# Rotary part of a two-layer encoder kernel: from its own stage into the projection, and semaphores cleared by five engines

## The chip, the cores and the metric

One Trainium2 chip, one core of it. The time is what the device takes for one execution of the whole program, in microseconds (us). The kernel before took 4610.36 us in the median of three runs (4608.76 to 4613.35).

## What is computed

Two layers of an encoder on 2048 tokens of 1024 features, in float32. Each layer normalises, projects to 26 x 128 columns (and 16 more), and sends the columns through a gated delta net (12 tiles after a convolution, 4 gate tiles) and through attention with 8 query heads over 2 key heads of 64 dimensions (4 tiles of queries, one of keys, one of values, 4 of gates). What matters here is what happens to queries and keys between projection and attention:

```python
def _rmsnorm(x, w):
    y = x32 * lax.rsqrt(jnp.mean(x32 * x32, axis=-1, keepdims=True) + EPS)
    return (y * w.astype(jnp.float32)).astype(x.dtype)

def _rope(x, pos):
    ...
    rot = jnp.concatenate([-x32[..., d // 2:], x32[..., :d // 2]], axis=-1)
    return (x32 * cos + rot * sin).astype(x.dtype)

def _axial_rope(x, row, col):
    h = x.shape[-1] // 2
    return jnp.concatenate([_rope(x[..., :h], row), _rope(x[..., h:], col)], axis=-1)

    q = _axial_rope(_rmsnorm(q, q_norm_w), row, col)
    k = _axial_rope(_rmsnorm(k, k_norm_w), row, col)
```

With d = 32 in `_rope`, the 64 dimensions of a head fall into four quarters of 16: quarter 0 is rotated with 1, quarter 2 with 3.

## The kernel before

The program (`build`, L2022) is a chain of stages. Each stage opens its semaphores, runs one block in which SP (DMA queue), TensorE, ScalarE, VectorE and GpSimd each have their own list of instructions, and closes with a barrier. Stages do not overlap: `semaphores` (L52) lets all engines come to the end of the block, then clears every semaphore of the stage one after the other on SP (L58), then holds a barrier over all engines (L59). A layer is `input_projection` (L162), `token_inputs` (L450), `delta_net`, `attention`, `output_projection`, `token_scales`.

**input_projection.** Weights and activations are split into a high and a low float32r part, and a tile of 128 output columns x 2048 tokens is the sum of three products: per half tile (1024 tokens) 8 x 3 x 2 matmuls of 512 columns (`tile_half`, L242). Tiles go in the order values, queries, keys of the delta net (tiles 0 to 11, with a convolution on VectorE), attention queries (12 to 15), keys (16), values (17), gates (18 to 25). For tile t+1 ScalarE casts the high part of the weights (`split_hi`, L309) and VectorE subtracts for the low part (`split_w`, L374), each once tile t-1 is done; the weights have two buffers. ScalarE evicts each half tile from PSUM (`evacuate`, L314; `plain`, L335), SP stores the tile to DRAM (L212, the last two L216) and loads the weights of tile t+2 (L210). For tiles 4 to 17 GpSimd squares the tile (L296) and TensorE sums the squares over the 64 dimensions of each head with 16 small matmuls (`square_sum`, L259), put between the matmuls of the second half of tile t+2; the squares have one buffer. At the end VectorE copies the sums to SBUF (L425).

**token_inputs** computes decay and beta tables of the delta net from `ba` (a chain of some 25 small operations, with four transposed pieces of `v` copied by ScalarE, L584, ahead of the logarithm, L587), stores `b_rows` (L507) and, after the rotary rows, `att_v` (L515). The rotary part runs behind it in the same lists. Inverse root mean squares are taken (L595, L689), transposed, stored as rows to DRAM and loaded again as two rows per tile (L510 to L513). Then for each of 5 tiles: TensorE swaps the quarters with a permutation (`swap_quarters`, L554), VectorE makes two products with the norm weight and the tables (L705, L708), GpSimd adds them (L523), TensorE spreads the inverse over 128 partitions (L570), VectorE scales (L719), ScalarE casts the high part (L612), VectorE subtracts the low part (L696), and ScalarE's queue issues four stores of 64 partitions (L605). The loads of these tiles (L505), the swap matrix and the tables (L500 to L503) are issued at the beginning of the stage.

## Time and profile before

| | |
|---|---|
| median of 3 runs | 4610.36 us |
| profiled execution: time | 4615.77 us |
| profiled execution: span of the instructions | 4614.0 us |
| mean granted TensorE clock | 0.934 |
| TensorE busy | 4031.0 us (87%) |
| VectorE busy | 2615.2 us (57%) |
| ScalarE busy | 1869.3 us (41%) |
| GpSimd busy | 726.8 us (16%) |
| DMA | 418.01 MB, mean 91 GB/s |

The profile is of one execution of the program. PE is TensorE's matmuls, PEld its weight loads, DVE VectorE, ACT ScalarE, POOL GpSimd, SPq the queue on which SP issues DMAs. L-numbers are lines of the kernel. "x16" is a count of instructions. What stands in brackets behind an instruction of a timeline is how long its engine was idle before it and who released it. PEclk is the granted clock of TensorE as a share of 2.4 GHz, so 0.50 is 1.2 GHz. The first layer's input_projection ends and its token_inputs begins at 743.76 us from the start of the span.

### The profile page before, as it was taken

To read this page: it belongs to the slowest core of one execution; us is meant where nothing else is said; L and a number is where in the kernel's file an instruction comes from. 1 tells how busy PE (TensorE), PEld (TensorE's weight loads), DVE (VectorE), ACT (ScalarE), POOL (GpSimd) and SP (SyncE) were. 2 spreads that over 40 slices of the span, in tenths; PEclk is the share of its full clock that TensorE was granted. 3 is DMA by queue.
4 is the path that set the end of the run, shared out by engine and by line. 5 is a ranking of instruction groups with operands and counts; after the bars stand their busy time and mean duration, and the time that the engine had idled before them with its cause. 6 is when DMAs were issued, how large, how long until landed. Compare 5 with 4: busy or idle time off the path is not lost. (4 is left out here: it accounts for less than half of the span.)

```text
span 4614.0 us, 57747 instructions
## 1 busy us (share of the span) xinstructions
PE 4031.0 (87%) x19861; PEld 3102.9 (67%) x19861; DVE 2615.2 (57%) x3176; ACT 1869.3 (41%) x2596; POOL 726.8 (16%) x770
## 2 busy tenths in 40 slices
PE   3999997569979999987879999856997999999693
PEld 2788884359956666656758888725996666666473
DVE  5543003457778888874255500045676888888532
ACT  3221111235547777761132211112453777777310
POOL 0011101478510000000000110035863000000000
PEclk9999997789989999998989999967998999999896
DMA  6111113744520000017231111265455000000635
GB/s 238 62 69 68 55 69 128 172 115 135 150 76 21 23 23 23 23 47 206 105 127 69 55 68 69 76 182 136 122 148 129 24 23 23 22 23 16 166 135 205
DMA packets 319745, 418.01 MB, mean 91 GB/s; under 512 B 104336, under 2 KB 254212, under 8 KB 292428
## 3 DMA queue, kind: packets, MB, share of 16 engines
q1 hardware_dynamic: 315232, 386.57, 26.9%
q10 hardware_dynamic: 4352, 29.36, 2.4%
q8 instruction: 92, 1.51, 0.1%
q14 instruction: 69, 0.57, 0.0%
HBM read 267.95 MB, written 147.91 MB: 90 GB/s over the span
## 5 line engine op out<-in xcount | busy, mean ns | idle before, releaser
L1687 DVE TENSOR_REDUCE att_sb_part<-att_banks 128x1 f32<-128x512 f32 x992 | 658.8, 685 | 150.7 <-PE att_banks L1572 142.6
L1675 ACT ACTIVATE att_sb_probs<-att_banks 128x1024 f32<-128x1024 f32 x512 | 524.9, 1025 | 379.3 <-PE att_banks L1598 379.1
L1705 DVE TENSOR_TENSOR att_sb_p_lo<-att_sb_probs,att_sb_p_hi 128x1024 fp32r<-128x1024 f32 x512 | 623.6, 1218 | 22.6 <-ACT att_sb_p_hi L1679 20.5
L1679 ACT ACTIVATE att_sb_p_hi<-att_sb_probs 128x1024 fp32r<-128x1024 f32 x512 | 543.3, 1061 | 16.2
L254 PE MATMUL proj_banks<-proj_sb_h_hi,proj_sb_w_hi 128*128 128x512 f32 x1600 | 518.3, 405 | 6.2 <-DVE proj_sb_w_lo L376 6.2
L254 PE MATMUL proj_banks<-proj_sb_h_lo,proj_sb_w_hi 128*128 128x512 f32 x1600 | 515.6, 403 | 0.0
L254 PE MATMUL proj_banks<-proj_sb_h_hi,proj_sb_w_lo 128*128 128x512 f32 x1600 | 515.5, 403 | 0.0
L376 DVE TENSOR_TENSOR proj_sb_w_lo<-proj_sb_w_raw,proj_sb_w_hi 128x1024 fp32r<-128x1024 f32 x52 | 69.2, 1330 | 640.8 <-ACT proj_sb_w_hi L312 640.8
L996 PE MATMUL dn_banks<-dn_sb_room 128*128 128x128 f32 x3072 | 379.8, 283 | 59.6 <-DMA dn_sb_room<-proj 28.3
L996 PEld LDWEIGHTS dn_banks<-dn_sb_room 128*128 128x128 f32 x3072 | 367.8, 198 | 82.2 <-DMA dn_sb_room<-proj 38.5
L1614 PE MATMUL att_banks<-att_sb_p_hi,att_sb_v_hi 128*65 128x512 f32 x1024 | 406.7, 397 | 12.7 <-DVE att_sb_o L1711 11.3
L1597 PE MATMUL att_banks<-att_sb_q,att_sb_k 128*128 128x512 f32 x1024 | 413.1, 403 | 2.8 <-DVE att_sb_q L1699 1.9
L296 POOL TENSOR_TENSOR proj_sb_sq<-proj_sb_out 128x2048 f32<-128x2048 f32 x28 | 100.8, 3600 | 1976.5 <-ACT proj_sb_out L333 1388.1
L1598 PE MATMUL att_banks<-att_sb_q,att_sb_k 68*128 68x512 f32 x1024 | 409.1, 399 | 0.0
L1614 PE MATMUL att_banks<-att_sb_p_hi,att_sb_v_lo 128*65 128x512 f32 x1024 | 404.3, 395 | 0.0
L1614 PE MATMUL att_banks<-att_sb_p_lo,att_sb_v_hi 128*65 128x512 f32 x1024 | 403.5, 394 | 0.0
L1572 PE MATMUL att_banks<-att_sb_k,att_sb_q 128*128 128x512 f32 x992 | 380.9, 413 | 7.2 <-DVE att_sb_part L1687 1.9
L254 PEld LDWEIGHTS proj_banks<-proj_sb_h_hi,proj_sb_w_hi 128*128 128x128 f32 x1600 | 289.4, 189 | 65.0 <-issue 7.1
L254 PEld LDWEIGHTS proj_banks<-proj_sb_h_hi,proj_sb_w_lo 128*128 128x128 f32 x1600 | 291.4, 189 | 60.7
L254 PEld LDWEIGHTS proj_banks<-proj_sb_h_lo,proj_sb_w_hi 128*128 128x128 f32 x1600 | 291.4, 189 | 60.7
L317 ACT ACTIVATE proj_sb_out<-proj_banks 128x1024 f32<-128x1024 f32 x56 | 57.4, 1026 | 566.1 <-PE proj_banks L254 566.1
L1572 PEld LDWEIGHTS att_banks<-att_sb_k,att_sb_q 128*128 128x128 f32 x992 | 189.1, 191 | 121.4 <-DVE att_sb_part L1687 65.7
(225 smaller groups left out, 5748.9 us busy)
## 6 DMA issues: line engine op xcount, KB each, us to landing
proj<-proj_sb_out SPq DMA_DIRECT2D x52, 1024.0 KB, 4.4
dn_sb_kq<-proj SPq DMA_DIRECT2D x64, 512.0 KB, 5.3
proj_sb_w_raw<-in_w_in SPq DMA_DIRECT2D x52, 516.0 KB, 5.2
dn_sb_room<-proj SPq DMA_DIRECT2D x32, 768.0 KB, 5.2
att_sb_q<-att_q SPq DMA_DIRECT2D x64, 256.0 KB, 2.9
out_sb_x<-x_res SPq DMA_DIRECT2D x16, 1024.0 KB, 7.0
x_res<-out_sb_x SPq DMA_DIRECT2D x16, 1024.0 KB, 4.1
out_sb_w_raw<-in_w_out SPq DMA_DIRECT2D x24, 512.0 KB, 4.9
```

Source lines behind the costliest of these rows:

```text
L254: mm = nc.tensor.matmul(ps[:, 2 * half + n, :], w[:, u, k, :], h[:, k, at:at + QB], start=(k == 0 and w is w_hi and h is h_hi), stop=(k == ...
L296: nc.gpsimd.tensor_tensor(sq[:], out[:, u, :], out[:, u, :], ALU.mult).then_inc(s["squared"], 1)
L376: nc.vector.tensor_tensor(w_lo[:, u].rearrange("p k m -> p (k m)"), w_raw[:, u, 0:KT * P], w_hi[:, u].rearrange("p k m -> p (k m)").bitcas ...
L996: mm = nc.tensor.matmul(out[:, h, :], left[:, h, :], right[:, h, :], start=True, stop=True)
L1572: nc.tensor.matmul(ps[:, 4 + u % 2, :], q1[:, slot, tile * P:(tile + 1) * P], k1[:, slot % 2, keys * QB:(keys + 1) * QB], start=True, stop ...
L1597: nc.tensor.matmul(out, k1[:, slot % 2, keys], q1[:, slot, :], start=True, stop=False)
L1598: mm = nc.tensor.matmul(out, k2[:, slot % 2, keys], q2[:, slot, :], start=False, stop=True)
L1614: mm = nc.tensor.matmul(ps[0:DH + 1, 6, :], part_v[:, kv, tile, :], part_p[:, at, m, :], start=opens, stop=(tile == NC - 1 and part_v is v ...
L1675: nc.scalar.activation(probs[:, pair % 2], ps[:, 2 * (pair % 2):2 * (pair % 2) + 2, :], ACT.Exp, scale=SCALE).then_inc(s["exp_done"], 1)
L1679: nc.scalar.activation(p_hi[:, pair % SLOTS], probs[:, pair % 2], ACT.Copy).then_inc(s["hi_done"], 1)
L1687: nc.vector.tensor_reduce(part[:, w // NQ, w % NQ:w % NQ + 1], ps[:, 4 + w % 2, :], AX.X, ALU.max) \
L1705: nc.vector.tensor_tensor(p_lo[:, pair % SLOTS], probs[:, pair % 2], p_hi[:, pair % SLOTS].bitcast(F32), ALU.subtract).then_inc(s["lo_done ...
```

## The change

1. The rotary part leaves `token_inputs` and goes into `input_projection`. The columns of queries and keys are laid out anew on the host: tile 12 holds quarters 0 and 2 of heads 0 to 3 and tile 13 their quarters 1 and 3, likewise 14 and 15 for heads 4 to 7, and 16 and 17 for the two key heads, whose upper 64 partitions hold half of the values each. A rotation then needs no permutation: it is between two tiles at the same partition.
2. A unit is 512 tokens of a pair of tiles; there are 3 pairs x 4 = 12 units. VectorE does all of it: four products, an addition, a scaling by rows broadcast from DRAM, a copy to the high part, a subtraction for the low part. Units 0 and 1 stand behind the weight split beside tile 20, then 3, 3, 2, 2 beside tiles 21 to 24. Inputs (`ab`, `inv`) and results (`xx`, `yy`) have two buffers each, in the space of `pad` and `sq`; the tables (`rope`) one.
3. SP stores and loads for the units between its weight loads and tile stores.
4. The square sums have four columns (one for each 32 partitions) in place of two. Those of tile 16 go between the matmuls of the first half of tile 18, those of tile 17 into its second half; the inverse roots are taken after tile 18, transposed by TensorE between the halves of tile 19, and stored and loaded as before.
5. `token_inputs` keeps the rest: 13 semaphores for 31. `input_projection` has 47 for 28.
6. In every stage the semaphores are cleared in turn by SP, VectorE, ScalarE, GpSimd and TensorE, each its own share.

```diff
+STATS = T_Z - T_Q
+QUARTER = P // 4
+PAIR_TILES = 3
+N_ROWS = ATT_HEADS + KV_HEADS
+ROPE_UNITS = PAIR_TILES * NQ
+ROPE_TILE = T_Z + 2
+UNITS_BESIDE = (2, 3, 3, 2, 2, 0)
+FIRST_BESIDE = (0, 2, 5, 8, 10, 12)
...
-        for s in sems.values():
-            nc.sync.sem_clear(s)
+        engines = (nc.sync, nc.vector, nc.scalar, nc.gpsimd, nc.tensor)
+        for n, s in enumerate(sems.values()):
+            engines[n % len(engines)].sem_clear(s)
...
+                def load_unit(n):
+                    if n >= ROPE_UNITS:
+                        return
+                    pair, at, parts = rope_unit(n)
+                    u = n % 2
+                    cols = slice(at, at + QB)
+                    if n >= 2:
+                        sp.wait_ge(s["scaled"], n - 1)
+                    sp.dma_start(ab[u][0:parts], a.proj[T_AQ + 2 * pair:T_AQ + 2 * pair + 2, 0:parts, cols]
+                                 .rearrange("f p t -> p f t")).then_inc(s[f"ab_loaded{u}"], 16)
+                    heads = parts // QUARTER
+                    sp.dma_start(inv[u][0:parts], a.qk_rows[4 * pair:4 * pair + heads, cols].unsqueeze(1)
+                                 .broadcast_to([heads, QUARTER, QB])).then_inc(s[f"inv_loaded{u}"], 16)
+
+                def load_rope(n):
+                    if n % PAIR_TILES == 0 and n < ROPE_UNITS:
+                        if n:
+                            sp.wait_ge(s["products"], n)
+                        cols = slice(rope_unit(n)[1], rope_unit(n)[1] + QB)
+                        sp.dma_start(rope, a.rope[:, :, cols].rearrange("f p t -> p f t")).then_inc(s["rope_loaded"], 16)
+
+                def store_unit(n):
+                    pair, at, parts = rope_unit(n)
+                    u = n % 2
+                    heads = parts // QUARTER
+                    dst = a.att_q[4 * pair:4 * pair + heads] if pair < PAIR_TILES - 1 else a.att_k
+                    for src, low in ((yy[u], 0), (xx[u], DH)):
+                        sp.wait_ge(s["lo" if low else "hi"], n + 1)
+                        for half in range(2):
+                            row = low + half * QUARTER
+                            sp.dma_start(dst[:, row:row + QUARTER, at:at + QB], src[0:parts, half, :]) \
+                                .then_inc(s[f"rope_stored{u}"], 16)
+
+                t = ROPE_TILE - 2
+                load_weights(t)
+                store_tile(t)
+                load_weights(t + 1)
+                sp.wait_ge(s["rows_copied"], 2)
+                rows_out = a.qk_rows.rearrange("r (c p) -> (r c) p", p=P)
+                sp.dma_start(rows_out[0:P], row_table[:, 0, :]).then_inc(s["rows_stored"], 16)
+                sp.dma_start(rows_out[P:N_ROWS * NC], row_table[0:N_ROWS * NC - P, 1, :]).then_inc(s["rows_stored"], 16)
+                sp.wait_ge(s["rows_stored"], 32)
+                load_rope(0)
+                load_unit(0)
+                load_unit(1)
+                for t in range(ROPE_TILE, N_TILES):
+                    load_weights(t)
+                    store_tile(t - 1)
+                    for n in range(FIRST_BESIDE[t - ROPE_TILE], FIRST_BESIDE[t - ROPE_TILE] + UNITS_BESIDE[t - ROPE_TILE]):
+                        load_rope(n + 1)
+                        store_unit(n)
+                        load_unit(n + 2)
+                store_tile(N_TILES - 1)
...
-                    col = (t - T_Q) * 2 * NC + 2 * n
-                    mm = nc.tensor.matmul(ps[:, 4, bass.ds(col, 2)], sq[:, n * P:(n + 1) * P], c.halves[:],
+                    col = (t - T_Q) * 4 * NC + 4 * n
+                    mm = nc.tensor.matmul(sums[:, bass.ds(col, 4)], sq[:, n * P:(n + 1) * P], c.quarters[:],
...
-                with pe.Fori(T_Q // 2 + 1, T_Z // 2 + 1) as i:
+                with pe.Fori(T_Q // 2 + 1, T_Z // 2) as i:
                     for u in range(2):
                         tile_half(i, u, 0)
 
-                        tile_half(i, u, 1, [lambda n=n: square_sum(i - 1, u, n) for n in range(NC)])
+                        tile_half(i, u, 1, [[lambda n=n: square_sum(i - 1, u, n)] for n in range(NC)])
+                i = T_Z // 2
+                tile_half(i, 0, 0, [[lambda n=n: square_sum(i - 1, 0, n)] for n in range(NC)])
+                late = [[]] * 12 + [[lambda n=n: square_sum(i - 1, 1, n)] for n in range(8)]
+                late += [[lambda n=n: square_sum(i - 1, 1, n), lambda n=n: square_sum(i - 1, 1, n + 1)] for n in range(8, NC, 2)]
+                tile_half(i, 0, 1, late)
+                tile_half(i, 1, 0)
+                pe.wait_ge(s["inv_rms"], 1)
+                nc.tensor.transpose(ps[:, 6, 0:P], rms_flat[:, 0:P], c.ident[:])
+                nc.tensor.transpose(ps[0:N_ROWS * NC - P, 7, 0:P], rms_flat[:, P:N_ROWS * NC], c.ident[:]) \
+                    .then_inc(s["turned"], 1)
+                tile_half(i, 1, 1)
...
+                plain(T_Z // 2, 0, ACT.Silu, True, True)
+                act.wait_ge(s["summed"], 2)
+                nc.scalar.activation(rms.rearrange("p m r c -> p m c r"), first_sums, ACT.Sqrt, bias=c.eps[:, 0:1],
+                                     scale=1.0 / DH).then_inc(s["root"], 1)
+                plain(T_Z // 2, 1, ACT.Silu, True, True)
+                for t in range(ROPE_TILE, N_TILES):
+                    plain(t // 2, t % 2, ACT.Silu, t + 1 < N_TILES)
...
+                def inverse_rms():
+                    att_sums = sums[:, (T_AQ - T_Q) * 4 * NC:STATS * 4 * NC] \
+                        .rearrange("p (m f c r) -> p m f c r", m=PAIR_TILES, f=2, r=4)
+                    dve.wait_ge(s["stats_done"], STATS)
+                    nc.vector.tensor_copy(first_sums, att_sums[:, :, 0]).then_inc(s["summed"], 1)
+                    dve.wait_ge(s["summed"], 1)
+                    nc.vector.tensor_tensor(first_sums, att_sums[:, :, 1], first_sums, ALU.add).then_inc(s["summed"], 1)
+                    nc.vector.tensor_reduce(c.sums[:].rearrange("p t c -> p (t c)"),
+                                            sums[:, 0:2 * DN_HEADS * 4 * NC].rearrange("p (n r) -> p n r", r=4),
+                                            AX.X, ALU.add).then_inc(s["edges"], 1)
+                    dve.wait_ge(s["root"], 1)
+                    nc.vector.reciprocal(rms_flat, rms_flat).then_inc(s["inv_rms"], 1)
+
+                def copy_rows():
+                    dve.wait_ge(s["turned"], 1)
+                    nc.vector.tensor_copy(row_table[:, 0, :], ps[:, 6, 0:P]).then_inc(s["rows_copied"], 1)
+                    nc.vector.tensor_copy(row_table[0:N_ROWS * NC - P, 1, :], ps[0:N_ROWS * NC - P, 7, 0:P]) \
+                        .then_inc(s["rows_copied"], 1)
+
+                def rope_products(n):
+                    pair, _, parts = rope_unit(n)
+                    u, k = n % 2, int(pair == PAIR_TILES - 1)
+                    w_first, w_second, w_negative = 2 * k, 2 * k + 1, 4 + k
+                    dve.wait_ge(s[f"ab_loaded{u}"], 16 * (n // 2 + 1))
+                    dve.wait_ge(s["rope_loaded"], 16 * (n // PAIR_TILES + 1))
+                    if n >= 2:
+                        dve.wait_ge(s[f"rope_stored{u}"], 64 * (n // 2))
+                    for dst, half, src, weight, table in ((xx, 0, 0, w_first, 0), (yy, 0, 1, w_negative, 1),
+                                                           (xx, 1, 1, w_second, 0), (yy, 1, 0, w_first, 1)):
+                        op = nc.vector.scalar_tensor_tensor(out=dst[u][0:parts, half, :], in0=ab[u][0:parts, src, :],
+                                                            scalar=qk_w[0:parts, weight:weight + 1],
+                                                            in1=rope[0:parts, table, :], op0=ALU.mult, op1=ALU.mult)
+                    op.then_inc(s["products"], 1)
+
+                def rope_rest(n):
+                    parts, u = rope_unit(n)[2], n % 2
+                    x, y = xx[u][0:parts], yy[u][0:parts]
+                    dve.wait_ge(s["products"], n + 1)
+                    nc.vector.tensor_tensor(x, x, y, ALU.add).then_inc(s["added"], 1)
+                    dve.wait_ge(s["added"], n + 1)
+                    dve.wait_ge(s[f"inv_loaded{u}"], 16 * (n // 2 + 1))
+                    factor = inv[u][0:parts].unsqueeze(1).broadcast_to([parts, 2, QB])
+                    nc.vector.tensor_tensor(x, x, factor, ALU.mult).then_inc(s["scaled"], 1)
+                    dve.wait_ge(s["scaled"], n + 1)
+                    nc.vector.tensor_copy(y.bitcast(F32R), x).then_inc(s["hi"], 1)
+                    dve.wait_ge(s["hi"], n + 1)
+                    nc.vector.tensor_tensor(x.bitcast(F32R), x, y, ALU.subtract).then_inc(s["lo"], 1)
+
+                split_w(T_Z + 1, 1)
+                inverse_rms()
+                split_w(T_Z + 2, 0)
+                copy_rows()
+                dve.wait_ge(s["qk_w_loaded"], 16)
+                nc.vector.tensor_scalar(qk_w[:, 4:6], qk_w[:, 1:4:2], -1.0, None, ALU.mult).then_inc(s["edges"], 1)
+                dve.wait_ge(s["edges"], 4)
+                for t in range(ROPE_TILE, N_TILES):
+                    if t + 1 < N_TILES:
+                        split_w(t + 1, (t + 1) % 2)
+                    for n in range(FIRST_BESIDE[t - ROPE_TILE], FIRST_BESIDE[t - ROPE_TILE] + UNITS_BESIDE[t - ROPE_TILE]):
+                        rope_products(n)
+                        rope_rest(n)
...
+                for kv in range(KV_HEADS):
+                    sp.dma_start(v[kv * DH:(kv + 1) * DH], a.proj[T_AK + kv, DH:P]).then_inc(s["v_loaded"], 16)
```

## Rows read from the trace of the kernel before

**Rows 1.** Windows: busy PE, PEld, DVE, ACT, POOL; clock; DMA; GB/s.
```profile
601.00:736.00 135.00, 135.00 (x578) 108.53 (x577) 6.67 (x6) 17.56 (x17) 0.00 (x0) 1.00 0.17 62
743.00:770.00 27.00, 10.47 (x44) 7.90 (x45) 9.55 (x30) 10.08 (x17) 0.00 (x0) 0.56 0.87 334
...
840.00:857.00 17.00, 0.00 (x0) 0.00 (x0) 0.00 (x0) 0.14 (x1) 0.14 (x1) 0.50 0.73 185
...
1400.00:1500.00 100.00, 98.88 (x418) 65.88 (x417) 88.58 (x115) 73.50 (x71) 0.00 (x0) 1.00 0.08 23
```

**Rows 2.** Timeline of SP's queue, first layer: start us, duration us, issue.
```profile
737.61 0.34 SPq L216 DMA_DIRECT2D proj<-proj_sb_out  x1
743.76 0.33 SPq L496 DMA_DIRECT2D tab_sb_ba<-ba  x1
...
745.51 0.42 SPq L499 DMA_DIRECT2D tab_sb_v<-proj  x1
...
762.79 0.33 SPq L507 DMA_DIRECT2D b_rows<-tab_sb_rows  x1
...
856.87 0.35 SPq L944 DMA_DIRECT2D dn_sb_masks<-in_masks  x1
```

**Rows 3.** The same, second layer.
```profile
2989.45 0.33 SPq L496 DMA_DIRECT2D tab_sb_ba<-ba  x1
...
3008.83 0.33 SPq L507 DMA_DIRECT2D b_rows<-tab_sb_rows  x1
...
3102.74 0.35 SPq L944 DMA_DIRECT2D dn_sb_masks<-in_masks  x1
```

**Rows 4.** Timeline of ScalarE in token_inputs.
```profile
755.76 0.58 ACT L584 COPY tab_sb_vt<-tab_banks 128x512 f32<-128x512 f32 x1 [0.24 <-PE tab_banks L536]
...
757.66 0.31 ACT L587 ACTIVATE tab_sb_ln<-tab_sb_u 128x128 f32<-128x128 f32 x1
```

**Rows 5.** Timeline of TensorE in token_inputs.
```profile
752.07 3.65 PE L536 MATMUL tab_banks<-c_ident,tab_sb_v 128*128 128x128 f32 x16 [1.27 <-DMA tab_sb_v<-proj]
...
766.62 0.48 PE L549 MATMUL tab_banks<-c_ident,tab_sb_att_inv 128*128 128x128 f32 x1 [4.38 <-DVE tab_sb_att_inv L689]
```

**Rows 6.** DMA issues: count, KB each, median us to landing.
```profile
dn_o<-dn_sb_room SPq DMA_DIRECT2D x32, 256.0 KB, 2.5
...
qk_rows<-tab_sb_rows SPq DMA_DIRECT2D x2, 64.0 KB, 1.7
```

**Rows 7.** The four last tile stores (L216), issue to landing.
```profile
DMA to landing us min/median/max: 3.8/3.9/3.9
```

**Rows 8.** Semaphore clears (L58): all, after input_projection, after token_inputs.
```profile
L58 SPq EVENT_SEMAPHORE_RANGE_CLEAR  x442: 25/25/35, 3.9 to 4613.7; - x148
...
L58 SPq EVENT_SEMAPHORE_RANGE_CLEAR  x28: 25/28/30, 741.9 to 743.5; - x28
...
L58 SPq EVENT_SEMAPHORE_RANGE_CLEAR  x31: 25/25/30, 854.8 to 856.6; - x31
```

**Rows 9.** Timelines: GpSimd, squares of tile 16; ScalarE, evictions.
```profile
545.45 3.60 POOL L296 TENSOR_TENSOR proj_sb_sq<-proj_sb_out 128x2048 f32<-128x2048 f32 x1 [22.33 <-PE proj_banks L265]
...
549.72 1.03 ACT L317 ACTIVATE proj_sb_out<-proj_banks 128x1024 f32<-128x1024 f32 x1 [13.66 <-PE proj_banks L254]
...
575.64 1.03 ACT L317 ACTIVATE proj_sb_out<-proj_banks 128x1024 f32<-128x1024 f32 x1 [13.58 <-PE proj_banks L254]
...
601.57 1.03 ACT L317 ACTIVATE proj_sb_out<-proj_banks 128x1024 f32<-128x1024 f32 x1 [13.58 <-PE proj_banks L254]
```

**Rows 10.** Instruction forms of VectorE: count, busy us, mean ns, idle.
```profile
L1705 DVE TENSOR_TENSOR att_sb_p_lo<-att_sb_probs,att_sb_p_hi 128x1024 fp32r<-128x1024 f32 x512 | 623.6, 1218 | 22.6 <-ACT att_sb_p_hi L1679 20.5
...
L416 DVE TENSOR_SCALAR proj_sb_out<-proj_sb_pad,proj_sb_taps 128x2048 f32<-128x2048 f32 x24 | 30.9, 1287 | 191.1 <-ACT proj_sb_pad L317 191.1
...
L708 DVE SCALAR_TENSOR_TENSOR tab_sb_q<-tab_sb_q,tab_sb_qk_w,tab_sb_rope 128x2048 f32<-128x2048 f32 x10 | 23.4, 2343 | 0.0
L1400 DVE SCALAR_TENSOR_TENSOR dn_sb_room<-dn_banks,dn_sb_norm,dn_sb_room 128x512 f32<-128x512 f32 x32 | 22.9, 748 | 38.3 <-PE dn_banks L1072 38.3
```

More of the change, by code:

```diff
@@ L166, in input_projection @@
              "conv_step taps_kept conv_done out_ready out_stored0 out_stored1 ba_hi ba_split ba_stored edges "
-             "squared stats_done")
+             "squared stats_done summed root inv_rms turned rows_copied rows_stored qk_w_loaded rope_loaded "
+             "ab_loaded0 ab_loaded1 inv_loaded0 inv_loaded1 products added scaled hi lo rope_stored0 rope_stored1")
     with ExitStack() as stack, semaphores(nc, names) as s:
@@ L212, in _, with load_weights, store_tile @@
                         sp.dma_start(a.proj[t], out[:, u, :]).then_inc(s[f"out_stored{u}"], 16)
+                def load_weights(t):
+                    if t + 2 < N_TILES:
+                        sp.wait_ge(s["w_lo"], t + 1)
+                        sp.dma_start(w_raw[:, t % 2, :], a.w_in[l, t + 2]).then_inc(s[f"w_loaded{t % 2}"], 16)
+                def store_tile(t):
+                    sp.wait_ge(s["out_ready"], t + 2)
+                    sp.dma_start(a.proj[t], out[:, t % 2, :]).then_inc(s[f"out_stored{t % 2}"], 16)
@@ L213, in _ @@
                 for u in range(2):
[L214 to L216 removed]
+                    sp.wait_ge(s[f"rope_stored{u}"], 64 * (ROPE_UNITS // 2))
                 for u in range(2):
@@ L250, in tile_half @@
                             if between:
-                                between.pop(0)()
+                                for extra in between.pop(0):
+                                    extra()
                             for n in range(2):
@@ L439, in scratch @@
     a.d_blk = dram("d_blk", (2, NC, N_DIR, DN_HEADS, N_BLK, BLK, BLK))
-    a.qk_rows = dram("qk_rows", (N_QK * 2, SEQ))
+    a.qk_rows = dram("qk_rows", (N_ROWS, SEQ))
     a.att_q = dram("att_q", (ATT_HEADS, P, SEQ))
@@ L450, in token_inputs @@
 def token_inputs(nc, a, c, l):
-    names = ("loaded ba_turned act_step dve_step summed g_copied turned copied stored att_root "
-             "const_loaded rows_loaded v_loaded v_turned v_copied v_stored swapped spread "
-             "cos_done sin_done rotated scaled hi lo stored0 stored1 " + " ".join(f"x_loaded{t}" for t in range(N_QK)))
+    names = "loaded ba_turned act_step dve_step summed g_copied turned copied stored v_loaded v_turned v_copied v_stored"
     n_ba = 2 * ITEMS
@@ L516, in _ @@
                 sp.wait_ge(s["v_stored"], 16)
-            @block.gpsimd
-            def _(pool):
-                for t in range(N_QK):
-                    pool.wait_ge(s["sin_done"], t + 1)
-                    pool.wait_ge(s["cos_done"], t + 1)
-                    nc.gpsimd.tensor_tensor(q[:, t, :], q[:, t, :], sin_part[:, t % 2, :], ALU.add).then_inc(s["rotated"], 1)
             @block.tensor
@@ L1984 @@
     pass
+FIRST_DIMS = [*range(0, DH // 4), *range(DH // 2, 3 * DH // 4)]
+SECOND_DIMS = [d + DH // 4 for d in FIRST_DIMS]
 def constants():
@@ L2034, in build @@
         c.eps = sb("c_eps", [P, 2])
-        c.halves = sb("c_halves", [P, 2])
-        c.sums = sb("c_sums", [P, T_Z - T_Q, NC, 2])
+        c.quarters = sb("c_quarters", [P, 4])
+        c.sums = sb("c_sums", [P, 2 * DN_HEADS, NC])
         c.tok = sb("c_tok", [P, TABLES, NC, ITEMS])
@@ L2068 @@
 _SHAPES = ["x_in", "w_in", "w_ba", "norm_w", "decay", "dn_norm_w", "qk_norm_w", "w_out",
-           "masks", "ident", "ones", "halves", "rope", "quarter", "swap", "halves_t"]
+           "masks", "ident", "ones", "quarters", "rope", "quarter"]
 def lay_out(x, norm_w, w_in, conv_w, a_log, dt_bias, dn_norm_w, q_norm_w, k_norm_w, w_out, final_norm_w):
@@ L2095, in lay_out @@
     g["dn_norm_w"] = np.asarray(dn_norm_w)[:, :, None]
-    swap = np.arange(DH).reshape(4, DH // 4)[[1, 0, 3, 2]].reshape(-1)
-    q, k = np.asarray(q_norm_w), np.asarray(k_norm_w)
-    g["qk_norm_w"] = np.stack([np.concatenate([v, v], axis=1) for v in (q, q[:, swap], k, k[:, swap])], axis=2)
+    norm_cols = []
+    for v in (np.asarray(q_norm_w), np.asarray(k_norm_w)):
+        first, second = np.tile(v[:, FIRST_DIMS], (1, 4)), np.tile(v[:, SECOND_DIMS], (1, 4))
+        norm_cols += [first, second]
+    g["qk_norm_w"] = np.stack(norm_cols, axis=2)
     g["w_out"] = np.asarray(w_out).reshape(depth, KT, P, KT, P).transpose(0, 3, 2, 1, 4).reshape(depth, KT, P, KT * P)
```

176 lines of the change are left out of this document (42 added, 134 removed).

## The prediction

> **What bounds the kernel now.** I read the windows first, to see which stage leaves TensorE idle. In the projection's last tiles TensorE is busy all of the 135 us at a clock of 1.00, VectorE 6.67 us and the DMA engines 17% [rows 1]. In the stage after it, the one that the change takes apart, TensorE has 10.47 us of work in the first 27 us at a clock of 0.56, and the last 17 us hold nothing but DMA [rows 1]. Then the SP queue's timeline, for the stage's length: it opens with the load of `ba` at 743.76 and the next stage's first issue is at 856.87, 113.1 us; in the second layer 2989.45 and 3102.74, 113.3 us [rows 2, 3]. The store of `b_rows`, the last thing that does not belong to the rotary part except the store of `att_v`, is issued 19.0 and 19.4 us after the start [rows 2, 3]. So some 94 us of each layer are rotary work and its stores, serial, with TensorE nearly idle, while VectorE idles beside the projection. The two layers run in sequence, so a microsecond off a stage is a microsecond off the time.
>
> **Part 1: the stage without its rotary part.** The b_rows store waits for a chain through ScalarE: the four copies of the turned `v` end at 755.76 + 0.58 and the logarithm follows at 757.66 [rows 4]. TensorE began to turn `v` at 752.07, after 1.27 us of waiting for its load, issued at 745.51 [rows 5, 2]. Without 7 MB of rotary loads on the queue, and with `v` in two halves issued back to back, I let that wait vanish: 1.1 us, and nearly 1.5 in the second layer. b_rows goes out at 17.9 us. It lands after some 1.9 us (the like-sized qk_rows store: 1.7 [rows 6]), at 19.8; SP only then issues `att_v`, 1 MB like a projection tile, whose last store lands in 3.9 us [rows 7]; with 0.3 for the wake-up of SP, 24.0. The last projection store shows what follows a landing: issued 737.61, landed 3.9 later, first semaphore clear at 741.9, so 0.4 us; the last clear at 743.5, the stage at 743.76, so 0.25 [rows 2, 7, 8]. With three clears in a row (below), 24.0 + 0.4 + 0.2 + 0.25 = 24.9 us. Saved: 88.2 + 88.4 = 176.6 us. Bounds: the stage takes no less than 23 us (`v` early by 2 us) and no more than 33 (both stores with 4 us more each, if what slowed them behind the rotary loads were not those loads): 160 to 180.
>
> **Part 2: the clears.** 31 clears span 854.8 to 856.6 and 28 span 741.9 to 743.5, 0.058 us each; 442 run in all [rows 8]. Other engines have stopped by then, so every one is on the path. After the change the projection has 47 names for 28 and the small stage 13 for 31; dealt to five engines and rounded up stage by stage, the longest share adds to 97. 345 fewer in series are 20.0 us, of which 2 x 28 x 0.058 = 3.2 are in part 1: 16.8 us. No row shows a clear on another engine. If TensorE's or GpSimd's took twice as long, the 97 cost 11.2 instead of 5.6; if they cost so much that nothing is won, 0. I take SP's pace, the only row, and keep 0 to 17.
>
> **Part 3: what the projection takes on.** TensorE: two transposes, 0.48 us for one [rows 5], between the halves of tile 19: 0.9 us a layer. The square sums stay 16 a tile; with them a tile takes 601.57 - 575.64 = 25.93 us [rows 9], without 22.5 (six tiles in the 135 us of [rows 1]), and four output columns for two I cost at nothing, between 0 and the 3.4 us that one tile's 16 sums add. They are earlier: tile 16's now start with tile 18. Its squares begin on GpSimd at 545.45 and take 3.60, so 549.05; tile 17's last eviction starts 549.72 [rows 9], so they are ready with under 0.5 us to spare; bound 0 to 0.5 a layer. Tile 17's squares follow at about 564, six us ahead of their first sum. inverse_rms: after tile 18, four small VectorE operations and a root with its table loads on ScalarE, some 5 us against 11.25 until the transposes: hidden under half a tile. Sum: 2 x 0.9 = 1.8 us, bounds 0 and 9.
>
> VectorE: a unit is four products of 512 columns, 0.75 us each (0.748, the nearest row, though it reads PSUM), two full-width operations and a subtraction of 1024, 1.22 each, and a copy of 1024, 0.69 (half of the single-source 1.287 for 2048) [rows 10]: 7.35 us. Twelve are 88 us, for 46 us of the same work in 2048-column operations (5 x 4 x 2.3) [rows 10]: smaller instructions cost more, but off the path.
>
> What covers it: unit 0 starts some 3.7 us into tile 20, behind the eviction, the ScalarE split and split_w(21). Three units and a split are 23.4 us, longer than a tile's 22.5, but split_w(t+1) is due only when tile t ends. split_w(23) stands behind five units: 3.7 + 5 x 7.35 + 1.3 = 42 us, w_hi at 48, due at 67.5. split_w(25) stands behind ten units and four splits: 83 us of work, due at 112.5. It holds until a unit costs (112.5 - 8.9) / 10 = 10.4 us, 8.9 being the 3.7 and four splits of 1.3 (1.22 and the start). SP: per unit three loads at most and four stores, seven DMAs at 0.35 to 0.6 us of issue; the load of weights t+2 and the store of tile t-1 stand in front of each tile's units, and the next ones behind them, so a late unit delays a weight load by a few us of the 16 it has (22.5 less its landing).
>
> DMA: a full unit moves 0.75 MB in and 1 MB out, eight full and four half ones, four rotary tables of 0.5 MB, and five tiles of 1.5 MB: 28 MB. The stores at 840 to 857 ran at 185 GB/s for a share of 0.73, 253 GB/s at full; the loads at 743 to 770 at 334 for 0.87, 384 at full [rows 1]. So 74 to 112 us of DMA beside 135 us of six tiles: tight at the lower rate, hidden at both, and the sum takes nothing for it. The Trainium skill (DMA: Bandwidth & Descriptors, "Bandwidth") speaks against 256 KB pieces: it asks for transfers of 1 MiB or more and gives each DMA about 2 us fixed, by itself an estimated 14 us for the seven of a unit. The rows say that what is fixed overlaps: 334 GB/s over 27 us with `v` and what follows issued half a microsecond apart. What the time would be if it did not is rival (d).
>
> **Sum.** 176.6 + 16.8 - 1.8 = 191.6 us off the profiled execution's 4615.8: 4424.2. That execution lies 5.4 us over the median of the runs, 4610.4, so I expect a median near 4420.
>
> **Rivals.**
> (a) The clears gain little, since other engines clear slowly or the barrier after them eats it: the change then does only part of what it says. Against it stand short semaphore instructions on all; for it, that no row shows one. 16.8 us back: 4437. 8%.
> (b) The delta net after the stage starts with another clock history: TensorE is idle for the last 17 us before it, at 0.50 [rows 1], so I expect the same start; a shift of 5 us a layer either way gives 4410 or 4430. 7%.
> (c) The units, not TensorE, set the end: the DMA chain of a unit (stores, then the next loads of the same buffers behind them in the queue) makes a unit cost 12 us for 7.35. Past 10.4 us each microsecond costs ten a layer: 2 x 16 = 32 us, 4452. For it: the 112 us above. 4%.
> (d) The queue takes one DMA at a time. With 2.5 us for a 256 KB store [rows 6] and 4 for the 0.5 MB load (the 1 MB store's 3.9 [rows 7]) a unit costs 16.5 us: 61 us a layer until tile 25 may start, 4542. Against it: the SP queue issued `v` and the loads behind it half a microsecond apart and 27 us ran at 334 GB/s [rows 1, 2]. 1%.
> (e) Slower: with VectorE, ScalarE, DMA and TensorE all busy in tiles 20 to 24 the granted clock falls to its lower level, 0.50. Five tiles of 22.5 us become 45: 225 us in both layers, 4645. It turns the gain into a loss from 95 of the 112.5 us of a layer at half clock. Against it: attention has TensorE 98.88 and VectorE 88.58 busy of 100 us at 1.00 [rows 1]. 2%.
>
> **How the numbers follow.** The forecast, units hidden and clears at SP's pace, has 78%. Its own range is 4410 to 4434: at its low end the stage takes 23 us and nothing is taken on (197 us off), at its high end half of the distance to each upper bound is used up (168 + 14 - 5, 177 off). The range that holds eight in ten reaches to (a) with a stage some us longer: 4406 to 4444. A measurement of this kernel tells 0.2%, 9 us, from no change. Only (e) and accidents reach there: faster 0.97, same 0.01, slower 0.02.
>
> **What would show it.** In the profile after: the small stage 23 to 27 us from its first issue to the next stage's; VectorE over 70% busy in tiles 20 to 24 while TensorE stays at 100% and 1.00; evictions there still 11.25 us apart; SP with at most 17 clears in the largest stage. I am wrong in the mechanism if TensorE waits there for w_lo or the spacing grows; wrong in a size if the stage stays above 30 us or clears on another engine run for over 0.1 us each.

## The result, and the profile after

| | before | changed |
|---|---|---|
| median | 4611.85 us (4608.76 to 4613.75, 4 runs) | 4552.77 us (4548.33 to 4555.85, 4 runs) |
| ratio | | 0.9868, interval 0.9854 to 0.9883 |
| profiled execution: span | 4614.0 us | 4551.2 us |
| mean granted TensorE clock | 0.934 | 0.936 |
| TensorE / VectorE busy | 4031.0 / 2615.2 us | 3938.0 / 2696.9 us |

Faster, by 59 us or 1.3%, well outside the spread of the runs. I forecast 190 us and a range that ended at 4444; the result lies more than 100 us above it.

The SP queue of the changed kernel, first layer and then second, gives the stages (start us, duration us, issue; L644 opens the small stage, L989 the delta net):

```profile
779.38 2.98 SPq L253 DMA_DIRECT2D proj<-proj_sb_out  x2
797.06 0.33 SPq L644 DMA_DIRECT2D tab_sb_ba<-ba  x1
...
817.49 0.33 SPq L650 DMA_DIRECT2D b_rows<-tab_sb_rows  x1
819.04 0.33 SPq L653 DMA_DIRECT2D att_v<-tab_sb_vt  x1
823.86 0.34 SPq L989 DMA_DIRECT2D dn_sb_masks<-in_masks  x1
...
3016.02 0.33 SPq L644 DMA_DIRECT2D tab_sb_ba<-ba  x1
...
3044.14 0.34 SPq L989 DMA_DIRECT2D dn_sb_masks<-in_masks  x1
```

Against [rows 2, 3] the span divides like this:

| us | first projection ends | small stage 1 | between | small stage 2 | rest |
|---|---|---|---|---|---|
| before | 743.8 | 113.1 | 2132.6 | 113.3 | 1511.3 |
| changed | 797.1 | 26.8 | 2192.2 | 28.1 | 1507.1 |
| difference | +53.3 | -86.3 | +59.6 | -85.2 | -4.2 |

The small stages gave 171.5 of the 176.6 us forecast. The two projections (the second lies in "between") took 113 back, where I had written 1.8. So it is the term of the projection that failed (what the clears give lies inside these figures; e4 measures it). Where inside the projection, the windows show (columns as in [rows 1]):

```profile
600.00:620.00 20.00, 20.00 (x87) 16.07 (x86) 15.27 (x17) 1.70 (x2) 0.00 (x0) 1.00 0.36 130
660.00:700.00 40.00, 28.47 (x122) 22.37 (x120) 19.55 (x21) 4.01 (x4) 0.00 (x0) 0.89 0.42 151
700.00:750.00 50.00, 26.68 (x100) 21.05 (x101) 23.55 (x26) 2.99 (x3) 0.00 (x0) 0.74 0.40 139
```

For 20 us all is as forecast: TensorE full at 1.00, VectorE at three quarters. From 660 to 750 TensorE is busy some 60% of the time, and VectorE half of it: neither is the bound. The DMA engines show 40% of their time and 140 to 150 GB/s, which looks like room to spare. ScalarE's timeline says what is late:

```profile
654.72 1.03 ACT L422 ACTIVATE proj_sb_out<-proj_banks 128x1024 f32<-128x1024 f32 x1 [9.06 <-PE proj_banks L348]
665.91 1.03 ACT L422 ACTIVATE proj_sb_out<-proj_banks 128x1024 f32<-128x1024 f32 x1 [10.16 <-PE proj_banks L348]
688.83 1.04 ACT L417 CAST proj_sb_w_hi<-proj_sb_w_raw 128x1024 fp32r<-128x1024 f32 x1 [21.90 <-DMA proj_sb_w_raw<-in_w_in]
...
736.01 1.05 ACT L417 CAST proj_sb_w_hi<-proj_sb_w_raw 128x1024 fp32r<-128x1024 f32 x1 [42.77 <-DMA proj_sb_w_raw<-in_w_in]
...
769.82 1.03 ACT L422 ACTIVATE proj_sb_out<-proj_banks 128x1024 f32<-128x1024 f32 x1 [29.40 <-DMA proj<-proj_sb_out]
```

Evictions are 11.2 us apart until 665.91. Then ScalarE sits idle 22 and 43 us until the load of a weight tile lands and it can be split, and 29 us until the store that frees the buffer of an eviction has landed. TensorE waits 34.9 us for the low part of the weights, which comes behind that split. VectorE's units show the same. The first took 7.15 us, from its start to the next one's. Later VectorE waits nine times for inputs of a unit, 72 us in all, and 43.8 us of that are three waits for the rotary table; two of them are shown:

```profile
601.92 0.75 DVE L559 SCALAR_TENSOR_TENSOR proj_sb_pad<-proj_sb_pad,proj_sb_qk_w,proj_sb_small 128x512 f32<-128x512 f32 x1
...
609.07 0.75 DVE L559 SCALAR_TENSOR_TENSOR proj_sb_pad<-proj_sb_pad,proj_sb_qk_w,proj_sb_small 128x512 f32<-128x512 f32 x1
...
645.42 0.75 DVE L559 SCALAR_TENSOR_TENSOR proj_sb_pad<-proj_sb_pad,proj_sb_qk_w,proj_sb_small 128x512 f32<-128x512 f32 x1 [13.89 <-DMA proj_sb_small<-in_rope]
...
692.62 0.75 DVE L559 SCALAR_TENSOR_TENSOR proj_sb_pad<-proj_sb_pad,proj_sb_qk_w,proj_sb_small 128x512 f32<-128x512 f32 x1 [15.02 <-DMA proj_sb_small<-in_rope]
```

Why the loads are late stands in SP's queue. An issue takes some 0.4 to 0.6 us for one DMA when the queue takes it freely (a line with "x2" is two in a row); here they stretch:

```profile
607.92 1.22 SPq L285 DMA_DIRECT2D att_q<-proj_sb_sq  x2
609.19 1.80 SPq L285 DMA_DIRECT2D att_q<-proj_sb_pad  x2
611.04 2.75 SPq L263 DMA_DIRECT2D proj_sb_pad<-proj  x1
...
632.82 2.24 SPq L285 DMA_DIRECT2D att_k<-proj_sb_sq  x2
635.10 9.70 SPq L285 DMA_DIRECT2D att_k<-proj_sb_pad  x2
```

```profile
proj<-proj_sb_out SPq DMA_DIRECT2D x6, 1024.0 KB, 12.9
...
proj_sb_w_raw<-in_w_in SPq DMA_DIRECT2D x3, 516.0 KB, 12.4
```

The first store of a unit is issued at 607.92, and by the third unit two 128 KB stores occupy SP for 9.7 us. The queue is backed up from its far end: a tile store lands after 12.9 us (second fence: the DMA view from 600 to 797; count, KB each, median us to landing), where it took 3.9 before [rows 7]. A queue that is full while its 16 engines are busy 40% of the time suggests that the work is not spread over the 16. Short windows show it directly:

```profile
619.00:625.00 6.00, 6.00 (x28) 4.81 (x27) 1.81 (x3) 2.08 (x2) 0.00 (x0) 1.00 0.26 99
699.00:705.00 6.00, 0.00 (x0) 0.00 (x0) 1.48 (x2) 0.00 (x0) 0.00 (x0) 0.50 0.25 84
736.00:739.00 3.00, 2.09 (x9) 1.34 (x8) 0.00 (x0) 1.57 (x2) 0.00 (x0) 1.00 0.12 49
```

In the first two SP is issuing stores of queries, in the third stores of keys. A share of 0.25 is 4 engines of 16, full, and one of 0.12 is 2; per engine that makes 21 to 25 GB/s. In the second of them TensorE does nothing at all.

What is peculiar to the new DMAs is their shape. A store goes to `dst[:, row:row + 32, cols]`: outermost are 4 heads (2 for the keys), then 32 rows. The load of the inverse roots is a broadcast, also with 4 or 2 outermost. Before, a store went to 64 rows of one head. The Trainium skill ("DMA: Bandwidth & Descriptors", section "Why a DMA increments its semaphore by 16 and not by 1") says that a DMA is spread over the largest number up to 16 that divides the outermost dimension of both sides, and over the lowest-numbered engines. For these stores that is 4 for the queries and 2 for the keys, and the shares of 0.26 and 0.12 agree. The trace does not number the engines, so which ones they are no run here shows. The rule was in reach when I predicted and I did not apply it.

The clears of the changed kernel, after the first delta net (the window 1250 to 1254):

```profile
L73 POOLq EVENT_SEMAPHORE_RANGE_CLEAR  x17: 38/38/38, 1251.2 to 1252.2; - x17
L73 ACTq EVENT_SEMAPHORE_RANGE_CLEAR  x17: 41/41/43, 1251.2 to 1252.3; - x17
L73 SPq EVENT_SEMAPHORE_RANGE_CLEAR  x17: 25/25/25, 1251.2 to 1252.1; - x17
L73 DVEq EVENT_SEMAPHORE_RANGE_CLEAR  x17: 54/54/56, 1251.3 to 1253.0; - x17
L73 PEldq EVENT_SEMAPHORE_RANGE_CLEAR  x16: 56/56/56, 1251.3 to 1253.1; - x16
```

SP's pace is 0.056 us (0.9 us for 16 steps), VectorE's 1.7/16 = 0.11 and TensorE's 1.8/15 = 0.12. If the longest share goes by VectorE's pace, it comes to an estimated 97 x 0.11 = 10.7 us.

### The profile page after: what moved, and what is told of

Its sections match the earlier page's. It is cut to its first block and busy times, and to the rows that moved or that the text cites. A ratio compares the mean times of both kernels' runs of the same rounds, so it can differ in the third digit from the quotient of the medians.

```text
span 4551.2 us, 57469 instructions
## 1 busy us (share of the span) xinstructions
PE 3938.0 (87%) x19701; PEld 3070.6 (67%) x19701; DVE 2696.9 (59%) x3334; ACT 1856.8 (41%) x2590; POOL 671.2 (15%) x760
## 5 line engine op out<-in xcount | busy, mean ns | idle before, releaser
L1659 PE MATMUL att_banks<-att_sb_p_hi,att_sb_v_hi 128*65 128x512 f32 x1024 | 406.4, 397 | 12.6 <-DVE att_sb_o L1756 11.2
```

The costliest lines, as they stand in the source:

```text
L1659: mm = nc.tensor.matmul(ps[0:DH + 1, 6, :], part_v[:, kv, tile, :], part_p[:, at, m, :], start=opens, stop=(tile == NC - 1 and part_v is v ...
```

## The experiments

Theory A: the stores and the loads of the inverse roots run on 4 or 2 of the 16 engines, because 4 or 2 entries are outermost, and those engines set the pace of the stage. Theory B: what costs is the number, the size or the plain volume of the added DMAs on one queue. Theory C, in two of the expectations, is that the broadcast load of the inverse roots alone holds the queue. e1, e2, e3 and e7 change only the form of those DMAs in the changed kernel, e5 the layout too. The kernel before ran beside them: 4608.41 us (7 runs) beside e1, e2, e3 and e5, and 4607.97 us (12 runs) beside e4, e6, e7 and e9. Ratios are to these. Differences to the changed kernel's 4552.77 are between medians; by the ratios they are 2 to 8 us smaller.

**e1: the stores into rows in a line.** The rows of a store are contiguous in one dimension of 128 (or 64); the places are not those of the heads, so attention reads other data, and the roots are made 100 times larger so that its exponentials stay small.

```diff
+                    dst = dst.rearrange("h p t -> (h p) t")
...
-                            row = low + half * QUARTER
-                            sp.dma_start(dst[:, row:row + QUARTER, at:at + QB], src[0:parts, half, :]) \
+                            row = (2 * (low > 0) + half) * parts
+                            sp.dma_start(dst[row:row + parts, at:at + QB], src[0:parts, half, :]) \
...
-                                     scale=1.0 / DH).then_inc(s["root"], 1)
+                                     scale=1e4 / DH).then_inc(s["root"], 1)
```

> The four stores of a unit keep their number, bytes and 2 KB rows, but the destination is 128 (64) rows in a line instead of 4 (2) heads x 32 rows, so that its outermost size is 128. Rows land in the wrong place, and the roots are taken 100 times larger so that the scores stay finite. Theory A (a DMA is spread over as many of the 16 engines as its outermost size on both sides allows: 4 and 2 in the change): the first two engines carry 2.5 MB in place of 5.0 MB over these tiles, which at 22 to 25 GB/s each is 100 to 113 us, under the 135 us of six tiles; TensorE no longer waits and the time falls from 4553 to 4430 to 4440. Theory B (256 KB transfers of 2 KB rows, seven to a unit, are slow whatever their shape): 4553, unchanged. Theory C (the broadcast load of the inverse roots is what holds the queue): 4553, unchanged.

Measured: 4435.98 us (4429.58 to 4437.28), ratio 0.9625 [0.9609, 0.9641]. The same bytes in as many DMAs of the same sizes and 2 KB pieces, and 117 us less: volume, number and size are excluded as the main cause, and so is theory C, which expected 4553. The rows do land at other places in DRAM here; e7 below, with the places unchanged, excludes these too.

**e2: the inverse roots alone.** One row is broadcast to all 128 partitions in place of four rows to 32 each (heads 1 to 3 of a tile get head 0's factors).

```diff
-                    sp.dma_start(inv[u][0:parts], a.qk_rows[4 * pair:4 * pair + heads, cols].unsqueeze(1)
-                                 .broadcast_to([heads, QUARTER, QB])).then_inc(s[f"inv_loaded{u}"], 16)
+                    sp.dma_start(inv[u][0:parts], a.qk_rows[4 * pair, cols].partition_broadcast(parts)) \
+                        .then_inc(s[f"inv_loaded{u}"], 16)
```

> Only the load of the inverse roots changes: one row broadcast to 128 (64) partitions in place of 4 (2) rows broadcast to 32 each, with the same bytes, so every head is scaled by the first head's roots. Theory A: the first two engines carry 4.4 MB for 5.0, 13% less, and the stretch of the units shrinks by some 24 us a layer: 4500 to 4510. Theory B: 4553. Theory C: near 4435.

Measured: 4506.64 us (4498.32 to 4521.56), ratio 0.9786 [0.9761, 0.9811]: 46 us less (38 by the ratios), with the stores still narrow. That is in theory A's range and far from the 4435 of theory C.

**e3: both edits, and the roots as in e1.**

> Both edits together: rows land in the wrong place, every head is scaled by the first head's roots, and the roots are taken 100 times larger. Theory A: the bytes spread over all engines, 74 to 87 us of DMA beside 135 us, 4425 to 4440, little or nothing under the run with the stores alone. Theory B: 4553.

Measured: 4434.11 us (4430.96 to 4439.35), the ratio of e1. Once the stores are wide, the narrow loads cost nothing: what counts is whether the busiest engine is done in time, not each DMA by itself.

**e5: the whole computation, interleaved.** The columns are laid out so that partition 4r + h of a tile holds dimension r of head h. The outermost dimension of stores and broadcasts is then the 32 rows, the heads stand inside. The key tiles carry the values in two head places beside the two key heads, and the units take these places along; `v` is loaded in four pieces. Cut here: tables, norm weights, key columns and the load of `v`, which follow the layout.

```diff
-                            sp.dma_start(dst[:, row:row + QUARTER, at:at + QB], src[0:parts, half, :]) \
+                            sp.dma_start(dst[:, row:row + QUARTER, at:at + QB].rearrange("h r t -> r h t"), src[:, half, :]) \
...
-                    sp.dma_start(inv[u][0:parts], a.qk_rows[4 * pair:4 * pair + heads, cols].unsqueeze(1)
-                                 .broadcast_to([heads, QUARTER, QB])).then_inc(s[f"inv_loaded{u}"], 16)
+                    sp.dma_start(inv[u], a.qk_rows[4 * pair:4 * pair + 4, cols].unsqueeze(0)
+                                 .broadcast_to([QUARTER, 4, QB])).then_inc(s[f"inv_loaded{u}"], 16)
...
-            parts += [at_q + h * DH + np.array(dims) for h in range(head, head + 4)]
+            parts += [at_q + h * DH + np.array([d]) for d in dims for h in range(head, head + 4)]
```

> A full computation: partition 4r + h holds dimension r of head h (before: 32h + r), so the stores go to 32 rows x 4 heads and the roots come as 32 (repeated) x 4 rows, with 32 outermost. The key pair takes 128 partitions like the others, values included, which adds 3.5 MB. Theory A: 4425 to 4445, TensorE at 100% beside the units, evictions 11.25 us apart. Theory B: 4553 or a little more, for the added bytes.

Measured: 4431.53 us (4423.46 to 4434.91), ratio 0.9615 [0.9599, 0.9631]. Its window, two issues of SP, and what landed from 600 to 744:

```profile
600.00:735.00 135.00, 135.00 (x578) 108.53 (x577) 90.27 (x101) 17.58 (x17) 0.00 (x0) 1.00 0.67 230
```
```profile
611.69 1.29 SPq L285 DMA_DIRECT2D att_q<-proj_sb_sq  x2
613.02 1.27 SPq L285 DMA_DIRECT2D att_q<-proj_sb_pad  x2
...
744.40 0.33 SPq L644 DMA_DIRECT2D tab_sb_ba<-ba  x1
```
```profile
proj<-proj_sb_out SPq DMA_DIRECT2D x7, 1024.0 KB, 4.8
...
att_q<-proj_sb_sq SPq DMA_DIRECT2D x16, 256.0 KB, 2.5
...
proj_sb_w_raw<-in_w_in SPq DMA_DIRECT2D x3, 516.0 KB, 6.2
```

TensorE is busy in all 135 us at 1.00 beside 90 us of VectorE, the picture forecast; a 256 KB store lands in 2.5 us and the small stage begins at 744.40, 0.6 us later than before the change. It moves more bytes than the changed kernel (the two extra head places of the key units) and takes 121 us less.

**e6: the narrow shape in the kernel before.** Another stage, another queue (ScalarE's), larger DMAs:

```diff
-                    for half in range(2):
-                        head = (2 * t if t < N_QK - 1 else 0) + half
-                        part = slice(half * DH, (half + 1) * DH)
-                        for src, at in ((hi, 0), (lo, DH)):
-                            act.dma_start(dst[head, at:at + DH], src[part, t % 2, :].bitcast(F32)) \
-                                .then_inc(s[f"stored{t % 2}"], 16)
+                    head = 2 * t if t < N_QK - 1 else 0
+                    for src, at in ((hi, 0), (lo, DH)):
+                        act.dma_start(dst[head:head + 2, at:at + DH], src[:, t % 2, :].bitcast(F32)) \
+                            .then_inc(s[f"stored{t % 2}"], 16)
```

> The kernel before, where only the rotary stores differ: the two heads of a tile go out in one DMA of 1 MB (destination 2 heads x 64 rows) in place of two of 512 KB; half as many DMAs, twice as large, same bytes, same 8 KB pieces. Theory A (a DMA whose outermost dimension has 2 entries runs on 2 of the 16 engines): 10.5 MB a layer over two engines at 22 to 25 GB/s each are 210 to 240 us from about 790 us on, where the stage ended at 857; 140 to 170 us more a layer, 4890 to 4950. Theory B (the number or the size of DMAs is what costs): the same or a little faster than before, 4600 to 4612.

Measured: 4906.36 us (4905.0 to 4912.14), ratio 1.0648 [1.0632, 1.0664]; the stage takes 262.3 us for 113.1. Half as many DMAs of twice the size make the kernel 298 us slower. The window of its stores, where nothing else moves, and then the same stretch of the kernel before:

```profile
800.00:1000.00 200.00, 20.00 (x30) 7.07 (x28) 23.25 (x11) 6.04 (x4) 11.56 (x3) 0.52 0.12 52
```
```profile
800.00:857.00 57.00, 22.61 (x35) 8.01 (x33) 24.89 (x11) 7.42 (x5) 14.87 (x4) 0.59 0.80 184
```

A share of 0.12 is 2 engines of 16, full; 52 GB/s are 26 for each of them. The rule of the Trainium skill named above ("DMA: Bandwidth & Descriptors", the same section) gives 2 for this shape, and the trace agrees.

**e7: the layout kept, the DMAs cut by head.** Each has 32 rows outermost, 64 KB; a full unit has 21 DMAs in place of 6, and the output is whole.

```diff
-                    sp.dma_start(inv[u][0:parts], a.qk_rows[4 * pair:4 * pair + heads, cols].unsqueeze(1)
-                                 .broadcast_to([heads, QUARTER, QB])).then_inc(s[f"inv_loaded{u}"], 16)
+                    for h in range(heads):
+                        sp.dma_start(inv[u][h * QUARTER:(h + 1) * QUARTER],
+                                     a.qk_rows[4 * pair + h, cols].partition_broadcast(QUARTER)) \
+                            .then_inc(s[f"inv_loaded{u}"], 16)
...
-                            sp.dma_start(dst[:, row:row + QUARTER, at:at + QB], src[0:parts, half, :]) \
-                                .then_inc(s[f"rope_stored{u}"], 16)
+                            for h in range(heads):
+                                sp.dma_start(dst[h, row:row + QUARTER, at:at + QB],
+                                             src[h * QUARTER:(h + 1) * QUARTER, half, :]) \
+                                    .then_inc(s[f"rope_stored{u}"], 16)
```

> The changed kernel, its layout kept; each store of a unit and each load of inverse roots is cut into one DMA per head (32 rows x 512, 64 KB), so that a full unit has 21 DMAs in place of 6. The output is whole. Theory A (fan-out): every DMA now has 32 entries outermost and runs on 16 engines; 21 issues of some 0.4 us are 8.4 us a unit, still under the 11 us that a unit may take: 4430 to 4450. Theory B (each DMA costs a fixed time on the queue, small ones are bad): more than three times as many DMAs make the stage longer than in the changed kernel, 4600 or more.

Measured: 4448.44 us (4442.38 to 4449.2), ratio 0.9646 [0.9631, 0.9661]: at the upper end of theory A's range, and 104 us faster than the changed kernel with more than three times as many DMAs, and with every row written to the same place. Of the 17 us to e5 some 13 lie in the two projections, where the issues take longer:

```profile
610.18 3.63 SPq L292 DMA_DIRECT2D att_q<-proj_sb_sq  x8
613.85 4.61 SPq L292 DMA_DIRECT2D att_q<-proj_sb_pad  x8
```

Sixteen stores take SP 8.2 us, twelve more than e5 issues, and weights behind them come late once more (ScalarE is idle 14.6 us before one split of the first layer, until the load lands); the small stage begins at 750.53, 6 us after e5's. The rest lies in the small stages and behind them and is not explained.

**e4: the clears alone, in the kernel before.**

```diff
-        for s in sems.values():
-            nc.sync.sem_clear(s)
+        engines = (nc.sync, nc.vector, nc.scalar, nc.gpsimd, nc.tensor)
+        for n, s in enumerate(sems.values()):
+            engines[n % len(engines)].sem_clear(s)
```

> The kernel before with nothing changed but the clears, dealt to five engines. My forecast, 345 clears less in series at SP's 0.058 us each: 20 us off, 4590. By the rows of the changed kernel, where VectorE and TensorE take 0.11 us for one: 25.7 us of clears before against some 10.7 now, 15 us off, 4595. Rival (a) of the prediction, nothing is won: 4608 to 4612.

Measured: 4597.26 us (4589.86 to 4605.61, 8 runs) against 4607.97, ratio 0.9978 [0.9967, 0.9988]: 10 us, between 5.5 and 15. That nothing is won (rival (a)) is excluded, and so are the 20 us of SP's pace on every engine; the 15 us that the slower engines' pace gives are at the edge of the interval.

**e9: e5 with another order in the small stage.**

```diff
+                sp.wait_ge(s["v_copied"], NQ)
+                sp.dma_start(a.att_v.rearrange("p c k d -> p c (k d)"), vt[:]).then_inc(s["v_stored"], 16)
                 sp.wait_ge(s["copied"], 1)
                 sp.dma_start(a.b_rows.rearrange("c i t -> (c i) t"), rows[:]).then_inc(s["stored"], 16)
                 sp.wait_ge(s["stored"], 16)
-                sp.wait_ge(s["v_copied"], NQ)
-                sp.dma_start(a.att_v.rearrange("p c k d -> p c (k d)"), vt[:]).then_inc(s["v_stored"], 16)
...
+                act.wait_ge(s["dve_step"], 6)
+                nc.scalar.activation(ln[:], u[:], ACT.Ln).then_inc(s["act_step"], 1)
                 for n in range(NQ):
                     act.wait_ge(s["v_turned"], n + 1)
                     nc.scalar.copy(vt[:, n * NQ:(n + 1) * NQ, :].rearrange("p c d -> p (c d)"), ps[:, NQ + n, :]) \
                         .then_inc(s["v_copied"], 1)
-                act.wait_ge(s["dve_step"], 6)
-                nc.scalar.activation(ln[:], u[:], ACT.Ln).then_inc(s["act_step"], 1)
```

> The interleaved version (e5) with another order in the small stage alone: ScalarE takes the logarithm before the four copies of v instead of behind them, and att_v is stored ahead of b_rows instead of after b_rows has landed. If the stage is set by the late v, the copies behind it and two stores in a row: b_rows goes out 4 to 5 us earlier, att_v 6 us earlier, the stage takes 19 to 21 us for 26.5: 11 to 15 us off e5's 4431, 4416 to 4420. Rival: the two stores side by side slow each other, or the logarithm's table load only moves: 4426 to 4431.

Measured: 4416.84 us (4412.88 to 4420.37), ratio 0.9581 [0.9568, 0.9594]; it is the fastest version, 3% under the changed kernel. Its SP queue in the small stage:

```profile
744.23 0.33 SPq L644 DMA_DIRECT2D tab_sb_ba<-ba  x1
...
758.08 0.35 SPq L653 DMA_DIRECT2D att_v<-tab_sb_vt  x1
760.00 0.34 SPq L655 DMA_DIRECT2D b_rows<-tab_sb_rows  x1
763.15 0.33 SPq L992 DMA_DIRECT2D dn_sb_masks<-in_masks  x1
```

The stage takes 18.9 us for e5's 26.5: b_rows goes out 15.8 us after the start for 20.0, and the large store is under way before it. Two orders were changed at once, so what each gives alone is not shown.

## Why the prediction was wrong, step by step

**The step that failed** is the paragraph on DMA in Part 3: "So 74 to 112 us of DMA beside 135 us of six tiles: tight at the lower rate, hidden at both, and the sum takes nothing for it". The term put at nothing cost some 111 us: the two projections came out 113 us longer for a forecast 1.8. The step divided 28 MB by rates that all 16 engines had reached together, in stretches whose DMAs had 64 or 128 rows outermost. The volume was right: 27.7 MB from 600 to 797. Its spread was not. On the busiest engine lie 262 KB of stores a unit (1 MB over 4 engines, or 512 KB over 2), 66 KB of inverse roots, and a sixteenth of the other 14.6 MB: 12 x 0.328 + 0.91 = 4.8 MB. At the 26 GB/s for one engine that e6 shows this is 186 us; from the first store of a unit to the end of the stage it took 607.9 to 797.1, 189. That these agree within 3 us is in part luck: at the 21 to 25 GB/s of the changed kernel's own short windows it would be 190 to 230 us. The same count at 26 GB/s gives 4.2 MB or 162 us for e2, whose stage ended at 779.8, 170 after its own first store at 610.2; and for e1 2.4 MB or 91 us, which 135 us of matmuls hide, as measured. That narrow DMAs are the cause is shown by taking them away (e1, e3, e5 and e7, and the loads alone in e2) and by putting them in elsewhere (e6). Whether they slow one another because they use the same engines, or because the queue works through them one after another, the runs do not tell apart: the count comes out alike.

**Rival (c)** had the mechanism: the DMAs, not TensorE, set the stage's end. I gave it 4% and 12 us a unit. Its sign came too, which I had named as showing the mechanism wrong: TensorE waited there for w_lo. The twelve units of the first layer started between 601.9 and 764.8, on average 14.8 us apart, and the weights behind them in the queue were held back with them. Rival (d), one DMA at a time with 16.5 us a unit, came near the measured time (4542 for 4553) for a wrong reason: in e5 the same number of DMAs on the same queue does not hold TensorE up. That agreement of a total would have misled; e5, and the shares of 0.26 and 0.12 in the short windows, tell the two apart. The 2 us fixed for each DMA, which Part 3 set under "Bandwidth", stand in the Trainium skill ("DMA: Bandwidth & Descriptors") in the section "Anatomy of one DMA — SWDGE (gpsimd) path", so for DMAs that GpSimd issues. The estimated 14 us a unit are not what SP's queue showed: in e5 the stores of the first two units start 7.2 us apart, at 611.7 and 618.9.

**Part 1**: 26.8 and 28.1 us for a forecast 24.9, 171.5 us for 176.6, inside its bounds. The step that fell is the wait for `v`. I let it vanish, as the rotary loads were gone. In the changed kernel it is longer: this is TensorE's row for [rows 5],

```profile
806.81 3.68 PE L667 MATMUL tab_banks<-c_ident,tab_sb_v 128*128 128x128 f32 x16 [2.75 <-DMA tab_sb_v<-proj]
```

which starts 9.8 us after the stage for 8.3 before, and b_rows goes out at 20.4 for the forecast 17.9; its landing was faster instead (1.5 us from issue to the next issue, for 1.9 and the wake-up). It is not the narrow DMAs' doing: where those are gone, the wait is still 3.3 to 3.6 us with `v` in two pieces (e1, e3, e7) and 2.7 and 2.5 us with `v` in four (e5, e9). `v` in one piece, as in the kernel before, was not tried in this stage; the cause stays open. That ScalarE's copies of `v` stood in front of the logarithm was in [rows 4] all along; I used it to carry `v` forward and went no further; in e9 b_rows goes out 4.2 us earlier without them, and with the stores in their new order the stage is 7.5 us shorter.

**Part 2**: mis-sized. I took SP's pace for all five engines; VectorE and TensorE need twice as long. The bound of 11.2 us for the longest share, which I gave and did not take, is near the 10.7 that the paces give; e4 gained 10 us, for my 20.

**Part 3, the rest**: right. The unit on VectorE, 7.15 us for 7.35; evictions 11.2 us apart while the weights came; the clock 1.00 beside all of it in e5, so rival (e) was wrong. In the changed kernel the clock fell to 0.50 after TensorE had stopped for want of weights (699 to 705 above), and stayed there for some us after it resumed; that is the 0.74 from 700 to 750. Of rival (b) nothing can be said within a few us: the rest after the second small stage was 1511.3 us before, 1507.1 after, 1499.1 in e5 and 1499.7 in e4, a spread as large as the shift in question.

**The forecast as a design** was nearly right: e5, the same change with wide DMAs, has a ratio of 0.9615, 4433 beside the 4610.4 that I started from, in the forecast's own range of 4410 to 4434 (its low end should read 4413: 4610 less the 197 us worked out for it). Of the 13 us to 4420, 3 are two small stages 1.6 us longer each and some 5 to 10 the clears; the rest, up to 5 us, is left open.

## What to carry to other kernels

Before adding up megabytes, read the outermost dimension of both sides of each DMA: with 2 or 4 entries there, the bytes lay on 2 or 4 engines here, in two stages and on two queues. Count as if every narrow DMA used the same few engines: narrow bytes over 2 or 4, the rest over 16. In a profile the sign is a queue whose issues stretch to several us and whose landings triple while the mean share of the 16 engines stays near 0.4, and at 0.25 or 0.12 in short windows; the cure is a layout that puts the long dimension outermost, or, a little dearer, one DMA for each entry.

## What the runs showed that I had not expected

- A narrow DMA holds up wide ones behind it on its queue: the weight load, with 128 partitions outermost, landed after 12.4 us in the changed kernel and 6.2 in e5.
- The narrow loads cost 38 to 46 us beside narrow stores (e2) and nothing beside wide ones (e1 and e3 within 2 us): costs of this kind do not add.
- Clearing one semaphore takes 0.056 us on SP but 0.11 to 0.12 on VectorE and TensorE.
